# Idle products on TensorE in the waits of three norms, ahead of the first up products

## The reference, cut to what matters

```python
def rms_norm(x, g):
    xf = x.astype(jnp.float32)
    y = xf * lax.rsqrt(jnp.mean(xf * xf, axis=-1, keepdims=True) + NORM_EPS)
    return (y * g.astype(jnp.float32)).astype(x.dtype)

for layer in range(DEPTH):
    h = rms_norm(x, g[0])
    mix = s5_mixer(h) if layer == 0 else mlstm_mixer(h)
    x = x + rms_norm(mix, g[1])
    f, fb = conv_ffn(rms_norm(x, g[2]), ...)   # up, conv, gelu(gate) * val, down
    x = x + rms_norm(f, g[3])
```

## Time and profile before

| | us |
|---|---|
| median of 3 runs | 3535.53 |
| lowest and highest of them | 3528.97, 3538.4 |
| the profiled execution, its own time | 3543.97 |
| its span in the profile | 3542.2 |
| mean granted clock of PE in it | 0.964 of full |

### The profile page before, as it was taken

One profiled execution on the slowest core, in us unless ns is written; L12 is line 12 of the kernel. 1 busy time (PEld: TensorE's weight loads), 2 busy tenths in 40 slices (PEclk: granted clock), 3 DMA queues, 4 the chain that ended last, 5 costly groups with the idle time before them and its releaser, 6 DMA issues. The chain is left out here.

```text
span 3542.2 us, 53423 instructions
## 1 busy us (share of the span) xinstructions
PE 3297.3 (93%) x20054; PEld 3164.9 (89%) x20054; DVE 1859.9 (53%) x2799; ACT 1171.8 (33%) x1909; POOL 512.1 (14%) x790
## 2 busy tenths in 40 slices
PE   5549989999999998999988999979999999999997
PEld 4439989999999998999986799979999999999997
DVE  8933554544444546322235666654555554555556
ACT  6232444223332233322244322224443222223222
POOL 2240001000000012000012333220011000000011
PEclk7669999999999999999999999999999999999999
DMA  3545531111111112333249522224534434334443
GB/s 86 144 121 141 164 110 44 47 43 39 44 42 42 42 61 100 116 108 108 102 147 322 185 82 75 83 87 132 163 110 147 128 125 132 124 122 134 132 134 127
DMA packets 400425, 389.38 MB, mean 110 GB/s; under 512 B 46164, under 2 KB 337304, under 8 KB 400088
## 3 DMA queue, kind: packets, MB, share of 16 engines
q1 hardware_dynamic: 374714, 324.06, 29.7%
q0 software_dynamic: 18336, 55.14, 4.7%
q10 hardware_dynamic: 7176, 7.35, 0.7%
HBM read 281.45 MB, written 102.63 MB: 108 GB/s over the span
## 5 line engine op out<-in xcount | busy, mean ns | idle before, releaser
L1251 PE MATMUL pair<-x_head,w_head 128*128 128x384 f32 x2544 | 860.5, 338 | 54.2 <-DVE w_rest L862 29.7
L1251 PE MATMUL pair<-x_rest,w_head 128*128 128x384 f32 x2544 | 856.6, 337 | 0.0
L1251 PE MATMUL pair<-x_head,w_rest 128*128 128x384 f32 x2544 | 856.4, 337 | 0.0
L1541 DVE SCALAR_TENSOR_TENSOR cv<-u,par,cv 128x1024 f32<-128x1024 f32 x176 | 225.6, 1282 | 647.3 <-ACT u L1482 647.0
L862 DVE TENSOR_TENSOR w_rest<-w_raw,w_head 128x1024 fp32r<-128x1024 f32 x260 | 317.6, 1222 | 464.3 <-ACT w_head L858 464.3
L1251 PEld LDWEIGHTS pair<-x_head,w_head 128*128 128x128 f32 x2544 | 482.5, 190 | 62.2 <-issue 46.2
L1251 PEld LDWEIGHTS pair<-x_rest,w_head 128*128 128x128 f32 x2544 | 482.7, 190 | 1.5
L1251 PEld LDWEIGHTS pair<-x_head,w_rest 128*128 128x128 f32 x2544 | 482.3, 190 | 0.0
L858 ACT ACTIVATE w_head<-w_raw 128x1024 fp32r<-128x1024 f32 x260 | 276.0, 1061 | 577.9 <-PE pair L1443 276.0
L1477 ACT ACTIVATE cv<-pair,par 128x384 f32<-128x384 f32 x264 | 177.2, 671 | 598.0 <-PE pair L1251 583.0
L1443 PE MATMUL pair<-a_head,w_head 128*128 128x384 f32 x1056 | 359.4, 340 | 8.9 <-DVE f L1574 7.2
(11 more groups left out here) (495 smaller groups left out, 4986.1 us busy)
## 6 DMA issues: line engine op xcount, KB each, us to landing
w_raw<-in_ffn_w_up_dram SPq DMA_DIRECT2D x88, 512.0 KB, 4.1
hs<-in_state_mlstm_C_dram SPq DMA_DIRECT2D x32, 1024.0 KB, 8.4
c_room<-in_state_mlstm_C_dram SPq DMA_DIRECT2D x64, 512.0 KB, 5.5
out_dram<-c_room SPq DMA_DIRECT2D x64, 512.0 KB, 4.6
w_raw<-in_s_w_glu_dram SPq DMA_DIRECT2D x48, 512.0 KB, 4.2
w_raw<-in_mlstm_w_down_dram SPq DMA_DIRECT2D x48, 512.0 KB, 4.2
w_raw<-in_ffn_w_down_dram SPq DMA_DIRECT2D x44, 512.0 KB, 3.8
w_raw<-in_mlstm_w_up_dram SPq DMA_DIRECT2D x32, 512.0 KB, 4.8
```

Source lines behind the costliest of these rows:

```text
L1251: m = pe.matmul(out[:, 0:TB], lhs[slot][:, P * k:P * k + P], rhs[:, k, TB * c:TB * c + TB], start=(k == 0 and q == 0), stop=(k == KD - 1 a ...
L1541: ins = dve.scalar_tensor_tensor(out=cp, in0=up[:, j:j + SEQ], scalar=tw, in1=cp, op0=ALU.mult, op1=ALU.add)
```

## The change

A new method `idle` issues `count` products of the identity with ones into the first 128 columns of bank 6. Nobody reads them, and they signal nothing. It is called at four places in PE's order: 10 of them behind the last glu tile of the first seam, ahead of the wait for `glu.gated` and `glu.free`; and 15 of them behind the spread of step 5 in each of the three seams, ahead of `first(0, 2)`. Nothing is removed or moved.

```diff
@@ class Norm, behind spread
+    def idle(self, pe, count):
+
+        for _ in range(count):
+            pe.matmul(self.env.bank[6][:, 0:P], self.env.ident[:, :], self.env.ones[:, :], start=True, stop=True)
@@ front, tensor, behind the loop over the glu tiles
                 if c and m in (2, 6):
                     norm1.spread(pe, g + m // 4)
+            norm1.idle(pe, 10)
             pe.wait_ge(glu.gated, steps)
             pe.wait_ge(glu.free, steps)
@@ front, tensor, first feed-forward net
             norm1.sums(pe, 5)
             norm1.spread(pe, 5)
+            norm1.idle(pe, 15)
             first(0, 2)
             first(1, 2)
             ffn_.tensor(pe)
@@ front, tensor, up projection
             norm2.sums(pe, 5)
             norm2.spread(pe, 5)
+            norm2.idle(pe, 15)
             first(0, 2)
             first(1, 2)
             pe.wait_ge(norm2.used, 6)
@@ back, tensor, second feed-forward net
             norm3.sums(pe, 5)
             norm3.spread(pe, 5)
+            norm3.idle(pe, 15)
             first(0, 2)
             first(1, 2)
             pe.wait_ge(norm3.used, 2 * NB)
```

## The result

The changed kernel takes 3553.25 us (median of 7 runs, 3548.66 to 3560.89), the kernel before 3538.4 (7 runs beside them, 3528.97 to 3543.8). The ratio is 1.0042, with an interval of 1.0029 to 1.0056: 15 us slower, where 1.4 us faster was forecast, and outside the range. The profiled execution took 3553.93 us with a span of 3552.2, so it lies 3553.93 - 3543.97 = 9.96 us over the one of before.

A forecast was written before the change was run, and what follows sets the result against it. PE, busy 93%, was taken to lose time at seam waits, as idle time and slow-clock products behind. Terms 2.86 + 0.12 + 0.66 + 0 - 2.23 = 1.41 us, off the median 3535.53, gave 3534.1 us; range 3526 to 3542.

The forecast's parts named there:

- Cost of the products themselves: Idle products at all four places end 0.8 to 0.9 us ahead of the release, so they cost nothing at full clock.
- the two signs of being wrong: The body behind norm3's seam starts earlier, counted from its spread, or the records of L1128 are 0.2 us apart.
- D: norm3's seam, ahead of `first(0, 2)`: gives 0; PE's wait grows to 2.98 us and a clock fall costs 2.23.
- the slower one: Rival: the idle products run at the low clock, overrun the waits by 8.6 us, old falls stay; 3544.1 us, chance 0.08.
- A: norm1's seam, ahead of `first(0, 0)`: its products take 4.21 us instead of 7.07 at full clock, a gain of 2.86.
- B: norm1's seam, ahead of `first(0, 2)`: only 0.12 us reaches ACT; PE's next wait grows to 1.79 us without a fall.
- C: norm2's seam, ahead of `first(0, 2)`: ACT is idle when the result comes, so the gain of 0.66 us passes.
- Does the clock stay up: At all four places the remaining waits of 0.8 to 0.9 us are short enough that the clock stays up.
- the two bounds: Price of the clock fall behind norm3's seam, bounded by 2.86 and 1.60 us; the middle, 2.23, was taken.

The follow-up runs named there:

- the run with 55: The kernel before with 55 idle products at the start of the last stage's PE block and none in any seam: 3553.79 us, ratio 1.0045.

## Why the prediction was wrong

**The step that failed** is "Cost of the products themselves": "Their cover is thus the wait itself, and they cost nothing, as long as they run at the full clock." The time that they take on PE was indeed covered. But they are also 220 instructions, and these moved the head of the second net's loop from place 34 to 254 of its piece: 17.9 us at the three jumps of the profiled execution, where the term was 0. The runs show it from three sides: the place alone brings the loss without the change, the change without the place loses nothing, and with 16 more instructions left in the piece the wait comes 16 instructions later. Neither of the two signs of being wrong that the prediction named came: at D the body starts 17.02 us behind the spread in both kernels, and the records of L1128 are 0.12 us apart. Both looked at the seams alone. No rival held this either; the slower one (idle products at half clock) was another mechanism, and it didn't occur: 20 records took 2.39 us and 30 took 3.51, 0.12 each.

That PE's stream comes in pieces is stated in the Trainium skill, Advanced Engine Details and Errata, "ISA Cache": lines of 16 KB, which it gives as 256 instructions, 32 KB of them and 128 KB on TensorE. The 16.4 KB a packet agree. By its 128 KB eight lines fit. The second net's loop, 1901 instructions in the compiled program, touches eight from place 34; yet before's trace has nine packets in each of the two passes between its jumps, so there the pieces are fetched anew in every pass, and whether the loop would fit decides nothing. Why they are isn't shown.

The other steps, by the profiled execution:

- **A** was forecast at 2.86 us. `first(0, 0)` took 4.26 instead of 7.07: 2.81. From there the whole seam moved, as said.
- **B**, 0.12: from the spread's end to the body it was 537.17 - (525.91 - 4.20) = 15.46, and is 530.19 - (514.04 + 0.94) = 15.21: 0.25. The wait ahead of the body is 1.54 (1.79 forecast), and the clock held.
- **C**, 0.66: from the spread's end to the next part's first products it was 14.23 and is 13.64, 0.59.
- **D**, 0 and a fall of 2.23: the body came no earlier, counted from its spread; the wait was 2.86 (2.98 forecast), the clock fell, and 24 products took 5.81 us, 1.6 more than 4.2. The lower of the two bounds was right, the middle was not.
- **Does the clock stay up**: yes, through rests of 0.78 to 0.94 us and the new waits of 0.6. The rule of the Trainium skill that was set against it (TensorE: Matmul & The Clock Gate, "A second HAM failure mode: psum-queue depth-cycling") isn't borne out at these seams.
- **Not forecast**: the wait of 2.27 us at norm2's seam stood there in after as well, and this time the clock stayed at 1.00 behind it, 1.6 us less. The stage ahead of A, which holds nothing of the change, was 3.9 us shorter, and the first net 1.5 us longer; both are left unexplained.

So the terms at the seams came to 2.81 + 0.25 + 0.6 - 1.6 = 2.1 us, forecast 1.4. The runs with the head elsewhere show what this is in the median: 1.1 us faster with nine products more, 0.7 slower with 17 at D, neither to be told from no change. With 57 calls, the run of 17 at D, the time lies in the forecast's range; with 55 it doesn't.

## What to carry to other kernels

An instruction that is hidden in time still takes room in the instruction stream, and everything behind it moves. Where a change adds or removes instructions ahead of a loop that one engine jumps back in, look at the three or four records behind each jump, before and after, at the jump's own record and at the packets of the instruction queue beside it. They say where the head falls, and check a count made elsewhere. If the loss is at the jumps, a few idle instructions ahead of the loop can undo it, as nine and two did here. A slowdown in a stage that wasn't edited is the sign to look for this.

## What the runs showed of the hardware beyond that

A jump back to a head with two instructions left in its piece cost PE 3.66 to 4.51 us each in the changed kernel, and some 2.6 us more in slow products; with 18 left there were 1.1 to 1.4 us behind the eight products and no slow ones, with 34 or more nothing that shows. The jump itself held PE's sequencer for 3.3 to 4.7 us at each of the second net's jumps, whatever the place. At two of the first net's three in the run with 55 it took 0.22 and 0.24 us, and there no packet started. A wait of about the same length need not have the same effect on the clock: 2.27 us at norm2's seam was followed by the lower level in before and not in after.
